# Feed-forward stages of a hybrid network by token halves, with the squares of the norm added by VectorE

## The reference

```python
def swiglu(x, w1, w3, w2):
    return (jax.nn.silu(x @ w1) * (x @ w3)) @ w2

for layer in range(DEPTH):
    hn = rmsnorm(h, attn_norm[layer])
    if layer % 2 == 0:
        h = h + hybrid_ab(hn, ...)        # ends in "@ w_out"
    else:
        h = h + nsa(hn, ...)              # ends in "@ w_out"
    h = h + swiglu(rmsnorm(h, ffn_norm[layer]), ffn_w1[layer], ffn_w3[layer], ffn_w2[layer])
return rmsnorm(h, final_norm)
```

## Time and profile before

| what | value |
|---|---|
| median of 3 runs | 3562.13 us (3561.63 to 3562.41) |
| the profiled execution | 3563.52 us |
| its span | 3561.8 us |
| mean granted clock of TensorE, share of full speed | 0.968 |
| TensorE busy | 3283.1 us, 92% |
| VectorE busy | 1825.6 us, 51% |
| ScalarE busy | 1280.3 us, 36% |
| DMA, mean over the span | 74 GB/s |

### The profile page before, as it was taken

One profiled execution on the slowest core, in us unless ns is written; L12 is line 12 of the kernel. 1 busy time (PEld: TensorE's weight loads), 2 busy tenths in 40 slices (PEclk: granted clock), 3 DMA queues, 4 the chain that ended last, 5 costly groups with the idle time before them and its releaser, 6 DMA issues. The chain is left out here.

```text
span 3561.8 us, 46967 instructions
## 1 busy us (share of the span) xinstructions
PE 3283.1 (92%) x19400; PEld 1860.6 (52%) x19400; DVE 1825.6 (51%) x2939; ACT 1280.3 (36%) x2226; POOL 65.6 (2%) x116
## 2 busy tenths in 40 slices
PE   6999989899999799999899978889998988889998
PEld 3566756666665366647454424334443455534443
DVE  5247566565533537676565466543323346643333
ACT  3234444344432224443344242332322235533221
POOL 0000011000000000011000000000000000000000
PEclk9999999999999999999999999999999989999999
DMA  6411010211122221110312222223223200012222
GB/s 282 150 50 40 32 45 33 81 38 45 42 107 71 78 72 37 62 51 19 108 54 100 99 71 71 83 71 107 91 98 117 83 24 1 1 71 95 107 85 81
DMA packets 47250, 263.03 MB, mean 74 GB/s; under 512 B 5656, under 2 KB 7320, under 8 KB 26432
## 3 DMA queue, kind: packets, MB, share of 16 engines
q1 hardware_dynamic: 46464, 256.89, 20.8%
q10 hardware_dynamic: 576, 3.15, 0.2%
HBM read 253.62 MB, written 4.19 MB: 72 GB/s over the span
## 5 line engine op out<-in xcount | busy, mean ns | idle before, releaser
L302 PE MATMUL banks<-h_sb,wsplit_sb 128*128 128x512 f16 (+2 forms) x7872 | 1604.9, 357 | 73.3 <-DVE h_sb L391 23.9
L302 PEld LDWEIGHTS banks<-h_sb,wsplit_sb 128*128 128x128 f16 x7872 | 759.8, 99 | 838.4 <-issue 174.5
L287 DVE SCALAR_TENSOR_TENSOR wsplit_sb<-ring_sb,wsplit_sb 128x1024 f16<-128x1024 f32 (+2 forms) x428 | 469.6, 1114 | 478.0 <-ACT wsplit_sb L277 476.0
L277 ACT ACTIVATE wsplit_sb<-ring_sb 128x1024 f16<-128x1024 f32 (+2 forms) x428 | 404.4, 962 | 718.7 <-PE banks L302 689.4
L302 PE MATMUL banks<-quads,wsplit_sb 128*128 128x512 f16 (+1 forms) x2880 | 601.6, 365 | 13.0 <-issue 8.9
L302 PEld LDWEIGHTS banks<-quads,wsplit_sb 128*128 128x128 f16 x2880 | 281.3, 98 | 312.1 <-issue 43.1
L302 PE MATMUL banks<-wsplit_sb,h_sb 128*128 128x256 f16 x2112 | 247.5, 274 | 2.6 <-DVE wsplit_sb L287 2.6
L302 PEld LDWEIGHTS banks<-wsplit_sb,h_sb 128*128 128x128 f16 x2112 | 206.1, 98 | 38.8 <-issue 9.8
L409 ACT ACTIVATE quads<-banks 128x512 f32<-128x512 f32 (+2 forms) x206 | 97.3, 474 | 325.5 <-PE banks L302 324.9
L496 PE MATMUL banks<-quads 64*128 64x256 f32 (+3 forms) x432 | 113.9, 514 | 1.8 <-PEq L86 1.6
L519 PE MATMUL banks<-work_sb,quads 128*128 128x128 f32 x832 | 106.8, 276 | 0.3 <-ACT work_sb L551 0.3
(11 more groups left out here) (326 smaller groups left out, 3178.8 us busy)
## 6 DMA issues: line engine op xcount, KB each, us to landing
ring_sb<-in_w_in SPq DMA_DIRECT2D x52, 1024.0 KB, 4.9
ring_sb<-in_w_ffn SPq DMA_DIRECT2D x44, 1024.0 KB, 4.8
ring_sb<-in_w_merge SPq DMA_DIRECT2D x48, 768.0 KB, 4.2
ring_sb<-in_w_ffn SPq DMA_DIRECT2D x32, 704.0 KB, 4.0
quads<-in_w_mod SPq DMA_DIRECT2D x12, 1024.0 KB, 26.2
x_sb<-in_w_mod SPq DMA_DIRECT2D x12, 1024.0 KB, 7.4
ring_sb<-in_w_ab SPq DMA_DIRECT2D x12, 1024.0 KB, 4.9
ring_sb<-in_w_nsa SPq DMA_DIRECT2D x10, 1024.0 KB, 4.9
```

The source lines that it names most:

```text
L277: act.activation(m.wsplit[:, g % 2, 0, half * n:half * n + n], m.ring[:, g % 2, half * n:half * n + n], ACT.Copy, scale=WSCALE).then_inc(w ...
L287: dve.scalar_tensor_tensor(m.wsplit[:, g % 2, 1, half * n:half * n + n], m.ring[:, g % 2, half * n:half * n + n], WSCALE, m.wsplit[:, g % ...
L302: mm = pe.matmul(p.bank, *p.terms(k, pw, px), start=(p.opens and k == 0 and z == 0), stop=(p.closes and k == p.depth - 1 and z == 2))
```

## The change

- The squares of a norm are no longer summed by eight products on TensorE. VectorE adds them (`Norm.additions`, L371 of the changed kernel), and one product with the ones matrix (L376) sums over partitions.
- A `Norm` has a span of tokens. In the feed-forward stages there are two, for tokens 0 to 255 and 256 to 511. The last two groups of the output projection, the first two feed-forward groups, and in layer 1 the last tile of the down projection, are computed for the first half of the tokens and then for the second. The final norm and its output are halved too.
- The planned times of the norm's steps change (1.4 for 1.25 us, in proportion to the span), for the norm in `nsa_project_window` too, which keeps 512 tokens.
- In the final norm the scales go through `Norm.scale` (L392); the pause of 11 us that was planned ahead of the feed-forward groups is gone.

```diff
@@ class Norm
-        self.squared, self.summed, self.steps, self.rooted, self.scaled, self.hi, self.lo = sems
+        self.squared, self.added, self.summed, self.steps, self.rooted, self.scaled, self.hi, self.lo = sems
+        self.a, self.b = span
+        self.c = (self.b - self.a) / S
...
+        self.sum = m.ps[:, bank, 0:self.b - self.a]
+        self.arrive = arrive or (lambda k: t0 - 6.5 + 0.7 * k)
...
     def squares(self, act):
         for k in range(KD):
             yield self.arrive(k)
-            if k >= 2:
-                act.wait_ge(self.summed, k - 1)
+            if k >= 3:
+                act.wait_ge(self.added, k - 2)
             if self.present:
                 act.wait_ge(*self.present(k))
-            act.activation(self.sq[k % 2], self.m.x[:, k, 0:S], ACT.Square).then_inc(self.squared, 1)
-        yield self.t0 + 5.0
+            act.activation(self.sq[k % 2] if k else self.rstd, self.x(k), ACT.Square).then_inc(self.squared, 1)
+        yield self.t0 + 6.0 * self.c
         act.wait_ge(self.steps, 2)
         act.activation(self.rstd, self.rstd, ACT.Sqrt).then_inc(self.rooted, 1)
 
+    def additions(self, dve):
+        for k in range(1, KD):
+            yield self.arrive(k) + 0.6
+            dve.wait_ge(self.squared, k + 1)
+            if k >= 2:
+                dve.wait_ge(self.added, k - 1)
+            dve.tensor_tensor(self.rstd, self.rstd, self.sq[k % 2], ALU.add).then_inc(self.added, 1)
+
     def sums(self, pe):
+        yield self.t0
+        pe.wait_ge(self.added, KD - 1)
+        pe.matmul(self.sum, self.m.ones[:, :], self.rstd, start=True, stop=True).then_inc(self.summed, 1)
+
+    def inverse(self, dve):
+        step = steps_of(dve, self.steps)
+        yield self.t0 + 1.9 * self.c
+        dve.wait_ge(self.summed, 1)
...
+    def scale(self, dve):
         for k in range(KD):
-            yield self.arrive(k) + 0.6
-            pe.wait_ge(self.squared, k + 1)
-            pe.matmul(self.m.ps[:, self.bank, :], self.m.ones[:, :], self.sq[k % 2], start=(k == 0), stop=(k == KD - 1)
-                      ).then_inc(self.summed, 1)
...
-            yield self.t0 + 5.7 + 1.25 * k
+            yield self.t0 + (6.6 + 1.4 * k) * self.c
...
     def halves(self, act):
         for k in range(KD):
-            yield self.t0 + 6.4 + 1.25 * k
+            yield self.t0 + (7.3 + 1.4 * k) * self.c
...
     def rest(self, dve):
         for k in range(KD):
-            yield self.t0 + 7.0 + 1.25 * k
+            yield self.t0 + (7.9 + 1.4 * k) * self.c
...
+EARLY, LATE = (0, S // 2), (S // 2, S)
...
+    parts = [residual_part(m, g0 + g, 2 * g + j, j, x, 0, S) for g in range(2) for j in range(2)]
+    for a, b in (EARLY, LATE):
+        parts += [residual_part(m, g0 + g, 2 * g + j, j, x, a, b) for g in range(2, 4) for j in range(2)]
@@ def ffn_window
         for i in range(KF // 2):
...
+            for a, b in spans if i == 0 else (LAT,):
+                silus = [up(i, 0, j, a, b) for j in range(2)]
+                gated = [up(i, 1, j, a, b) for j in range(2)]
...
+                if i == 0:
+                    silus[0].mate = True
+                parts += silus + gated
...
-        f1[0].pause, f1[0].mate = 11.0, True
...
+            for a, b in spans if n == KD - 1 and out is not None else (LAT,):
...
+        for c in range(2):
+            p = into[c]
+            norms.append(Norm(m, nsems[c], p[-1].t1 + 2.0, lambda k: vec(m, "ffn_norm", l * KD + k), m.h, 6 + c,
+                              norm_scratch(m, 2, c), lambda k, p=p: (dd, p[k].nth),
+                              arrive=lambda k, c=c, p=p: p[k].t1 + 0.7 + (0.5 * c if k < 4 else 0.0), span=spans[c]))
...
+            for f in finals:
+                for k in range(KD):
+                    sp.wait_ge(f.scaled, k + 1)
+                    sp.dma_start(out[:, k, f.a:f.b], m.x[:, k, f.a:f.b]).then_inc(written, 16)
```

More of the change, by code:

```diff
@@ new lines, in sums @@
+    def sums(self, pe):
+        yield self.t0
[5 more added lines that the diff above has]
+        dve.wait_ge(self.summed, 1)
+        step(dve.tensor_scalar(self.rstd, self.sum, 1.0 / D, EPS, ALU.mult, ALU.add))
+        step(dve.reciprocal(self.rstd, self.rstd))
+    def scale(self, dve):
+        for k in range(KD):
+            yield self.t0 + (6.6 + 1.4 * k) * self.c
@@ L401, in norm_scratch @@
-def norm_scratch(m):
+NORM = ("sq", "add", "sum", "st", "root", "scl", "nhi", "nlo")
+EARLY, LATE = (0, S // 2), (S // 2, S)
+def norm_scratch(m, pieces=1, n=0):
     e = m.E.rearrange("p u c -> p (u c)")
-    return [e[:, i * S:(i + 1) * S] for i in range(5)]
+    w = S // pieces
+    return [e[:, (5 * n + i) * w:(5 * n + i + 1) * w] for i in range(5)]
 def copy_to(out, func=ACT.Copy):
@@ L2095, in ffn_window @@
     hid = m.hidden
-    scratch = norm_scratch(m)
     HK = KF // 2
-    with stage(nc, *(f"ff_{q}" for q in DENSE + NORM + ("prod", "hhi", "hlo", "fsq", "fsum", "fst", "froot", "fscl", "fin", "outd"))) as (block, *sems):
+    spans = (EARLY, LATE)
+    own = [f"{q}{c}" for c in range(2) for q in NORM] + ["hhi", "hlo", "outd"]
+    own += [f"f{q}{c}" for c in range(2) for q in NORM[0:6]] if out is not None else []
+    with stage(nc, *(f"ff_{q}" for q in DENSE), *(f"ff_{q}" for q in own)) as (block, *sems):
@@ L2099, in ffn_window @@
         mm, da, dd = sems[0:3]
-        nsems, (made, hid_hi, hid_lo) = sems[3:10], sems[10:13]
-        fsems, (finished, written) = sems[13:18], sems[18:20]
+        nsems = sems[3:11], sems[11:19]
+        hid_hi, hid_lo, written = sems[19:22]
+        fsems = sems[22:28], sems[28:34]
         parts = residual_parts(m, g0, x)
-        into = list(parts)
+        into = [[parts[k] if k < 4 else parts[k + 4 * c] for k in range(KD)] for c in range(2)]
         products = []
-        silus = []
@@ new lines, in ffn_window @@
+        finals = []
+        if out is not None:
+            for c in range(2):
+                p = down[1::2][0:KD - 1] + [down[2 * KD - 1 + 2 * c]]
+                finals.append(Norm(m, (*fsems[c], None, None), p[-1].t1 + 2.0, lambda k: vec(m, "final_norm", k), None, 6 + c,
+                                   norm_scratch(m, 2, c), lambda k, p=p: (dd, p[k].nth),
+                                   arrive=lambda k, c=c, p=p: p[k].t1 + 0.7 + (0.5 * c if k < KD - 1 else 0.0), span=spans[c]))
@@ L2153, in halves_dve @@
                                   ).then_inc(hid_lo, 1)
-        if out is not None:
-            final = Norm(m, (*fsems, finished, finished), d.end + 2.0, lambda k: vec(m, "final_norm", k), None, 7, scratch,
-                         lambda k: (dd, closing[k].nth), arrive=lambda k: closing[k].t1 + 0.7)
-            def final_dve(dve):
-                step = steps_of(dve, final.steps)
-                yield final.t0
-                dve.wait_ge(final.summed, KD)
-                step(dve.tensor_scalar(final.rstd, m.ps[:, final.bank, :], 1.0 / D, EPS, ALU.mult, ALU.add))
-                step(dve.reciprocal(final.rstd, final.rstd))
-                dve.wait_ge(final.rooted, 1)
-                for k in range(KD):
-                    xk = m.x[:, k, 0:S]
-                    dve.scalar_tensor_tensor(xk, xk, final.gain(k), final.rstd, ALU.mult, ALU.mult).then_inc(finished, 1)
         @block.sync
@@ L2213, in nsa_project_window @@
         mm, da, dd = sems[0:3]
[L2214 to L2215 removed]
+        nsems = sems[3:11]
+        tables, cw_in, gw_in, rotated, roped, dup, hid_done, a_done, kv_done, v_done, kc_copied, kc_rot, gate_mm = sems[11:]
         tiles = [8, 10, 12, 14, 0, 2, 4, 6]
@@ L2371, in _ @@
         def _(dve):
-            weave(norm.scale(dve), norm.rest(dve), rope(dve), close_dve(dve), d.split_lo(dve), d.stores(dve, "dve"))
+            weave(norm.additions(dve), norm.inverse(dve), norm.scale(dve), norm.rest(dve), rope(dve), close_dve(dve), d.split_lo(dve), d.stores(dve, "dve"))
 def sparse_window(nc, m):
```

112 lines of the change are left out of this document (46 added, 66 removed).

## The result

The changed kernel took 3544.48 us (median of 5 runs, 3539.14 to 3546.20) against 3562.13: a ratio of 0.9945, 95% interval 0.9932 to 0.9958, or 17.7 us less. Run again among the experiments it took 3539.27 (6 runs) against 3562.17, ratio 0.9933 (0.9921 to 0.9945). The median of all eleven is 3540.2. I had forecast 3548.7, 13.4 us less. The profiled execution took 3539.89 us around a span of 3538.1, with a mean clock of 0.969.

What follows compares the result with a forecast made beforehand. TensorE, busy 92% of the span, and the 10.9 us norm gap were taken as the bound. Layer 0 -5.3, layer 1 -4.6, norm ahead of sparse stage +5.3, end -8.8: -13.4 from 3562.1 gives 3548.7 us, range 3540 to 3557.

Steps and rivals of the forecast that it cites:

- Part 1: Both layers' projections and the last down tiles: seven sums less on TensorE each time, minus 18.8 us; new sums 0.45 each.
- Part 2: Halves of 256 columns on TensorE: a pair takes 0.219 us against 0.216; plus 0.5, 0.5 and 0.2 us.
- Part 3: Gap between projection and feed-forward comes back in pieces: 12.0 us of TensorE idle per layer, against 10.9 before.
- all three pieces: TensorE idle per layer: 3.0 us before the first feed-forward product, 5.5 before the late sum, 3.5 among late features.
- my walk: Tracing the four queues in the new order, with durations from the old trace and 0.04 us per engine hand-over.
- Part 4: Lower granted clock behind the new 5.5 us idle in the feed-forward products: plus 1.4 us per layer, between 0 and 3.0.
- Part 5: 512-wide norm ahead of the sparse stage: the new order makes each feature take 2.18 us; plus 5.3 us.
- Part 6: End of kernel, last product to span's end: 12.3 us against 15.7, minus 3.4; includes 2.4 us of transfer.
- The promise: Rival: no TensorE idle between projection and feed-forward, -40 us in all, 3522 us; chance 4%.
- The 512-wide norm: Rival: the norm ahead of the sparse stage costs nothing, since later waits absorb it; 3543.4 us; chance 10%.
- Half operations: Slower rival: half operations cost what whole ones do, step 2.18 us rather than 1.4; 3572 us; chance 4%.
- A clock that stays low: Rival: the clock stays low after each broken stretch, 3.0 us more lost at three places; 3557.7 us; chance 18%.

Runs made afterwards that it cites:

- the filled run: Changed kernel plus products with unused results, 3 ahead of the first feed-forward product and 6 ahead of the late sum; 3546.1 us.
- the order alone: Changed kernel with only the 512-token norm's low parts 0.6 us later in the plan, so VectorE scales one feature ahead; 3537.2 us.
- all norms ahead: Changed kernel with low parts 0.6 us (0.3 for a half) later in the plan in all norms; 3535.9 us, again 3535.8.
- late sum behind the pair: Changed kernel with the late half's sum 2.8 us later in TensorE's plan, behind eight features of the early pair, not four; 3548.7 us.

## Why the prediction was right, and where its sizes were off

- **Part 1** (-18.8): right. The projection of layer 0 takes 45.15 us for 50.70, that of layer 1 42.28 for 48.05; the terms give -5.5 and -5.9, measured -5.6 and -5.8. The down tiles of layer 1 take 114.83 for 120.13, -5.3 as forecast. That additions cost nothing between the tiles is shown by doubling them.
- **Part 2**: right within those sums. With the last down tile whole the down tiles of layer 1 take 114.12 us, so its halves and their sum cost 0.7 (0.65 forecast).
- **Part 3** (12.0 of idle per layer): the mechanism right in all three pieces, the size too large. Late sum: 11.1 us behind the projection forecast, 9.3 measured; last feature: 27.6 forecast, 24.9 measured at full clock. I let VectorE begin an instruction 0.03 us behind the shown end of the one ahead. The earlier trace rows already had it otherwise: a scale at 2370.71, 0.75 long, and the next operation at 2371.38. Such a start is 0.08 before the shown end, so each VectorE operation that does not wait is 0.11 us too late in my walk. Twelve of them lie between layer 1's last projection product and its late sum, 1.3 us; with this taken off the same walk gives 9.8 and 25.4 (an estimate, the walk was not run as a kernel).
- The 0.478 that I took for a scale of 256 columns holds: 0.479 over 32 of them. The Trainium skill (VectorE: DVE Perf Modes, section on the trn2 errata) would have given an estimate of 0.33 by its table; the trace does not show that. The Trainium skill itself says in that section that this row of the table comes out too low. (With my own hand-overs 0.33 would make a pace of 1.17, not the 1.1 that I wrote.) The advice of the Trainium skill there, tiles of at least 512 elements, is half borne out: two halves cost VectorE 0.96 where a whole costs 0.75, and the halves gained all the same.

```profile
L392 DVE SCALAR_TENSOR_TENSOR work_sb<-x_sb,vecs_sb,work_sb 128x256 f32<-128x256 f32 x32 | 15.3, 479 | 1.1 <-ACT work_sb L363 1.1
```

- **Part 4** (+1.4 per layer): 1.0 in layer 0 and nothing in layer 1, by the filled run. My reason, that part of the loss falls where TensorE waits anyway, was right; in layer 1 all of it does, in layer 0 what delays the Silus does not.
- Parts 3 and 4 together: 29.0 us forecast from the projection to the last feature, 25.9 and 24.9 measured. These 3.1 and 4.1 us are all of the 2.9 by which layer 0 beat my number, and of the 3.6 of layer 1; small terms the other way make up the rest.
- **Part 5** (+5.3): +4.3. Place and cause right, since the order alone gives 4.2 back. The step is 2.06 us, not 2.18, by the same 0.11 per feature, 0.9 us over eight.
- **Part 6** (-3.4): -4.2. The last issue ends 9.4 us behind the last product, forecast 9.9, and 2.0 follow, not 2.4. For the writes, which the range allows for, no run shows an extra cost: in rows of 1 KB the span ends 2.0 us behind the last issue, where it was 2.4 in rows of 2 KB.
- **The sum.** The errors of the four stages all have one sign. One wrong habit, reading shown ends as the moment the engine is free, accounts for most of it in Parts 3 and 5; the clock of Part 4 (1.4 for 1.0 and nothing) and the transfer of Part 6 are errors of their own that happen to fall on the same side. The range held the median of the first five runs (3544.5) and of all eleven (3540.2, just so); that of the second six, 3539.3, lies below it.
- **Rivals.** The promise did not hold: TensorE idles 2.1 to 4.4 us at a time. The 512-wide norm cost what it was said to. Half operations cost 0.42 to 0.48, not 0.69 to 0.75. A clock that stays low did not come in the changed kernel, whose sparse attention took 0.3 us more than before; it came in four of the variants, and there in the sparse attention, where I had not looked for it.

## What to carry to other kernels

Two engines that hand each feature back and forth need the first of them one feature ahead; a table of planned times that puts each low part directly behind its scale takes that away, and gave back 3 to 4 us in each of three places here. An engine's idle time can be the symptom and not the cost: moving the late sum and filling the gap changed nothing in layer 1, while changing the order on the engine that it waited for gave 3.0. Where the idle engine itself sets the end, its clock does cost: 1.7 us per layer once the order was right. And once the changed stages repeat within 0.1 us, compare stages, since totals also carry what happens elsewhere.

## What was not expected of the hardware

- **Granted clock in an unchanged stage.** The sparse attention, the same instructions in all profiles, took 389.3 to 390.4 us in eight of them and 394.6 to 394.8 in the four of all norms ahead (twice), late sum behind the pair and idle filled. VectorE's and ScalarE's busy time there is the same, TensorE's 5 us longer at a lower clock; the same four have the slow start of layer 1's projection. Neither the chip nor the start of the stage decides it: each of the three chips of the experiments has profiles of both kinds, and the stage began at 2741.93 in the changed kernel (389.7) and in the filled one (394.6) alike. Each of two kernels that were profiled twice fell on its own side both times, which speaks for something in the kernel ahead of that stage. But chance is not ruled out: one execution of the filled kernel that was not profiled took 3536.3 us at a mean clock of 0.972, 10.3 less than the profiled one at 0.968, and the earliest start of the stages in any profile would explain only 1.5 of that. The cause stays open, and no run was made for it.
- **The clock costs by who waits.** The same low clock behind an idle of 2 to 4 us cost 0, 1.0 or 1.7 us, by whether VectorE's chain or TensorE set the end of the stretch.
- **VectorE starts early.** In the changed kernel's trace 930 of 3046 VectorE operations start before the shown end of the one ahead, nine in ten of them by 0.07 to 0.09 us.
